# Router of a mixture of experts: fewer, wider operations, another order before the branch, lower biases added at expert 24, flags read one at a time

## The reference, cut to what matters

```python
def moe(x, w_router, b_router, w_up, b_up, w_down, b_down):
    logits = (xt @ w_router + b_router).astype(jnp.float32)
    top_val, top_idx = lax.top_k(logits, TOP_K)
    gates = jax.nn.softmax(top_val, axis=-1).astype(x.dtype)
...
    def expert_block(args):
        tok, g, e = args
        hdn = x_pad[tok] @ w_up[e] + b_up[e]
        gate_h = jnp.minimum(hdn[:, :D_FF_2], SWIGLU_LIMIT)
        up_h = jnp.clip(hdn[:, D_FF_2:], -SWIGLU_LIMIT, SWIGLU_LIMIT)
        act = (up_h + 1.0) * gate_h * jax.nn.sigmoid(SWIGLU_ALPHA * gate_h)
        y = act @ w_down[e] + b_down[e]
        return y * g[:, None]
```

## Time and profile before

| | |
|---|---|
| median of 3 runs | 2517.97 us (2517.13 to 2519.25) |
| the profiled execution's own time | 2516.45 us |
| its span, first to last instruction | 2514.7 us |
| mean granted clock of TensorE | 0.981 |
| TensorE busy | 2357.4 us, 94% |
| VectorE busy | 594.2 us, 24% |
| ScalarE busy | 520.9 us, 21% |
| mean DMA rate | 239 GB/s |

### The profile page before, as it was taken

The page is one execution under the profiler, slowest core; times in us unless marked ns, Lnnn a source line. Parts: engine busy times, 40 slices in busy tenths (PEclk is TensorE's granted clock), DMA queues, the critical chain, the costliest instruction groups (busy, mean ns, idle before and its releaser), DMA issues.

```text
span 2514.7 us, 33890 instructions
## 1 busy us (share of the span) xinstructions
PE 2357.4 (94%) x14632; PEld 1725.4 (69%) x14632; DVE 594.2 (24%) x1698; ACT 520.9 (21%) x1223; POOL 45.9 (2%) x64
## 2 busy tenths in 40 slices
PE   6888999999999879999999978999999999999997
PEld 3676788888887667887868854565666555555556
DVE  2044410000005322001575321122222222222223
ACT  2254432210003333200444120111111111111112
POOL 0000200000000000000000000000000000000000
PEclk9999999999999989999999978999999999999999
DMA  8811321123323504444433446799999999999992
GB/s 341 334 68 39 118 77 69 67 72 133 152 79 134 201 34 188 146 165 151 152 133 131 188 183 273 296 426 427 426 427 427 427 426 427 426 427 426 427 427 99
DMA packets 42115, 601.61 MB, mean 239 GB/s; under 512 B 4672, under 2 KB 5184, under 8 KB 5600
## 3 DMA queue, kind: packets, MB, share of 16 engines
q1 hardware_dynamic: 41472, 593.30, 58.2%
q10 hardware_dynamic: 480, 5.97, 0.6%
HBM read 598.20 MB, written 1.05 MB: 238 GB/s over the span
## 4 chain that ended last, share of the span: by engine, by line
PE 79%; DMA 14%; DVE 3%; ACT 2%; issue 1%; POOL 0%; DVEq 0%; SPq 0%; POOLq 0%; PEldq 0%; ACTq 0%
PE PS L560 13%; PE PS L551 13%; PE PS L935 12%; PE PS L693 7%; PE PS L959 7%; DMA BIG<-in_w_up 6%; DMA RG<-in_w_up 6%; PE PS L442 4%; PE PS L541 3%; PE PS L877 2%; PE PS L971 2%; DMA SM<-in_w_up 1%; PE PS L498 1%; DMA RG<-in_w_ada 1%; PE PS L383 1%
## 5 line engine op out<-in xcount | busy, mean ns | idle before, releaser
L551 PE MATMUL PS<-HN,RG 128*128 128x256 f32 x1536 | 333.9, 380 | 4.0 <-ACT HN L1145 4.0
L560 PE MATMUL PS<-BIG,RG 128*128 128x256 f32 x1536 | 333.1, 379 | 0.0
L551 PEld LDWEIGHTS PS<-HN,RG 128*128 128x128 f32 x1536 | 292.8, 191 | 44.6 <-issue 4.6
L560 PEld LDWEIGHTS PS<-BIG,RG 128*128 128x128 f32 x1536 | 291.4, 190 | 42.8 <-issue 3.4
L935 PE MATMUL PS<-BIG,XS 128*64 128x256 f32 (+1 forms) x2016 | 236.7, 384 | 10.1 <-DMA BIG<-in_w_up 10.0
L935 PEld LDWEIGHTS PS<-BIG,XS 128*64 128x64 f32 (+1 forms) x2016 | 145.0, 138 | 100.1 <-issue 17.2
L1100 ACT ACTIVATE BIG<-PS 128x256 f32<-128x256 f32 (+1 forms) x247 | 102.4, 422 | 520.1 <-PE PS L551 243.8
L2008 DVE TENSOR_SCALAR STAT<-PS 128x128 f32<-128x128 f32 (+1 forms) x128 | 37.9, 296 | 679.1 <-PE PS L935 679.1
L935 PE MATMUL PS<-RG,XS 128*64 128x256 f32 (+1 forms) x1520 | 182.9, 391 | 8.5 <-DMA RG<-in_w_up 8.5
L693 PE MATMUL PS<-XS,RG 128*128 128x256 f32 x768 | 172.1, 382 | 5.0 <-DVE XS L1617 4.1
L935 PEld LDWEIGHTS PS<-RG,XS 128*64 128x64 f32 (+1 forms) x1520 | 110.1, 140 | 80.7 <-issue 18.0
(11 more groups left out here) (291 smaller groups left out, 2340.1 us busy)
## 6 DMA issues: line engine op xcount, KB each, us to landing
BIG<-in_w_up SPq DMA_DIRECT2D x64, 2048.0 KB, 31.7
RG<-in_w_up SPq DMA_DIRECT2D x48, 2048.0 KB, 32.3
RG<-in_w_ff SPq DMA_DIRECT2D x32, 2048.0 KB, 8.3
BIG<-in_w_down SPq DMA_DIRECT2D x32, 2048.0 KB, 33.2
RG<-in_w_ada SPq DMA_DIRECT2D x24, 2048.0 KB, 9.1
RG<-in_w_down SPq DMA_DIRECT2D x24, 2048.0 KB, 33.8
RG<-in_w_in SPq DMA_DIRECT2D x23, 2048.0 KB, 8.0
SM<-in_w_up SPq DMA_DIRECT2D x16, 2048.0 KB, 31.7
```

The lines of the kernel that those rows point to most:

```text
L551: m = pe.matmul(banks[b][:, 0:256], w[:, k, 128 * n:128 * n + 128], own(HN, s)[:, k, :], start=k == 0, stop=k == 7)
L560: m = pe.matmul(banks[b][:, 0:256], w[:, k, :], own(FFH, s)[:, k, :], start=k == 0, stop=k == 31)
```

## The change

- **Halves together.** VectorE takes both token halves in one operation of 64 elements where the operation allows; `max`, the scan and the tie-breaking operation are still issued per half, but with one wait for the two. ScalarE's two exponentials wait once.
- **Order on TensorE.** Behind the logits come the `ht` transposes, then `pos` (which waits for the masks alone), then the transposes of the gates. `lg`, `pos` and `gt` lie in banks 0 to 2, `ht` in 4 to 7. `pos` is four matmul calls instead of five: two of those against `MSK[:, 0]` are one with 64 columns.
- **First gather ahead of the branch.** `select(0)`, `gather(0)`, `gather_turn(0)` and ScalarE's evacuations of them stand ahead of the fork. VectorE makes the flags behind `select(0)`.
- **Lower biases.** The eight matmuls of L841 leave the router; the scatter of expert 0 now starts the accumulators, and the biases are added at the start of expert 24. (In `dense` they stay ahead of the experts.)
- **Flags.** Ahead of the fork each engine reads `over` and the flag of expert 0. At the start of each expert it reads the flag of the next, into one of two registers.

SyncE's and GpSimd's programs do not change. The core of the diff:

```diff
+            F.pool, F.turn = [0, 1, 2, 3], 0
             b = take(("lg",))
...
-            b = take(("gt",))
-            for tt in range(2):
-                pe.wait_ge(s_gts, tt + 1)
-                m = pe.transpose(banks[b][0:32, tt * 128:tt * 128 + 128], GTE[:, tt, :], ID2)
-            read_out(("gt",))
-            for d in range(8):
-                pe.matmul(accap(d), BD[0:32, d * 128:d * 128 + 128], GTT, start=d % 2 == 0, stop=False, skip_group_check=True)
+            pos_bank, gt_bank = take(("pos",)), take(("gt",))
             F.pool, F.turn = [4, 5, 6, 7], 0
...
+            pe.wait_ge(s_sm3, 48)
+            pe.wait_ge(s_msk, 1)
+            b = pos_bank
+            pe.matmul(banks[b][:, 0:32], TRI, MSK[:, 0, :], start=True, stop=True)
+            pe.matmul(banks[b][:, 32:96], ONE1, MSK[:, 0:1, :].broadcast_to([128, 2, 32]), start=True, stop=False)
+            pe.matmul(banks[b][:, 32:64], TRI, MSK[:, 1, :], start=False, stop=False)
+            pe.matmul(banks[b][:, 64:96], ONE1, MSK[:, 1, :], start=False, stop=True).then_inc(s_full[b], 1)
+            b = gt_bank
+            pe.wait_ge(s_gts, 1)
...
+            def biases():
+                for d in range(8):
+                    pe.matmul(accap(d), BD[0:32, d * 128:d * 128 + 128], GTT, start=False, stop=False, skip_group_check=True)
             def expert(ex, broad):
+                if ex + 1 < NEXP:
+                    pe.load(wide[(ex + 1) % 2], FLAG[0:1, ex + 1:ex + 2])
+                if ex == BIASES:
+                    biases()
+            for tt in range(2):
+                for half in range(2):
+                    read_out(("ht", tt, half))
+            gather(0)
+            pe.wait_ge(s_flag, 1)
+            read_out(("pos",))
+            read_out(("gt",))
+            pe.load(over, FLAG[0:1, 32:33])
+            pe.load(wide[0], FLAG[0:1, 0:1])
+            gather_turn(0)
             pe.br_cmp(over, 0, on_true="pe_sparse", on_false="pe_dense", comp_op="IS_EQ")
```

and on VectorE:

```diff
-            for tt in range(2):
-                step(dve.max(M8[:, tt, :], LGT[:, tt, :]))
...
+            for tt in range(2):
+                D.up(dve.max(M8[:, tt, :], LGT[:, tt, :]))
+            dve.wait_ge(s_dve, D.n)
+            dve.tensor_scalar(c4b[:, :, 2:3], v1, -1.0, None, ALU.mult).then_inc(s_rmx, 1)
+            step(dve.tensor_tensor(MSK, LGT, v4, ALU.is_gt))
+            D.up(dve.tensor_reduce(c4b[:, :, 0], MSK, AX.X, ALU.add))
+            step(dve.tensor_tensor(EQ, LGT, v4, ALU.is_equal))
+            D.up(dve.tensor_scalar(c4b[:, :, 1:2], c4b[:, :, 0:1], -1.0, 4.0, ALU.mult, ALU.add))
...
+            dve.tensor_tensor(MSK, MSK, EQ, ALU.add).then_inc(s_msk, 1)
+            dve.wait_ge(s_rex, 2)
...
+            b = full(("pos",))
+            step(dve.tensor_copy(SV[:, 0:64], banks[b][:, 0:64]))
+            select(0)
...
```

More of the change, by code:

```diff
@@ L856, in _ @@
                     m.then_inc(s_full[b], 1)
[L857 to L860, removed]
+            pe.wait_ge(s_sm3, 48)
[8 more added lines that the diff above has]
+            for tt in range(2):
+                m = pe.transpose(banks[b][0:32, tt * 128:tt * 128 + 128], GTE[:, tt, :], ID2)
+            m.then_inc(s_full[b], 1)
+            wide = [pe.alloc_register(f"pe_wide{i}") for i in range(2)]
             over = pe.alloc_register("pe_over")
-            pe.load(wide, FLAG[0:1, 0:32])
-            pe.load(over, FLAG[0:1, 32:33])
             ended = list(F.at)
@@ L970, in expert @@
                             lh = YV[rows, c * 256 + (j // 2) * 128:c * 256 + (j // 2) * 128 + 128]
-                        m = pe.matmul(accap(d), lh, SCT[rows, :], start=False, stop=ex == NEXP - 1, skip_group_check=True)
+                        m = pe.matmul(accap(d), lh, SCT[rows, :], start=ex == 0 and d % 2 == 0, stop=ex == NEXP - 1,
+                                      skip_group_check=True)
                 m.then_inc(s_scat, 1)
@@ L1010, in _ @@
             with nc.body("pe_sparse", valid_engines=[mybir.EngineType.PE]):
-                for tt in range(2):
-                    for half in range(2):
-                        read_out(("ht", tt, half))
-                gather(0)
-                gather_turn(0)
                 ahead = []
@@ L1072, in _ @@
             with nc.body("pe_dense", parent=fork, valid_engines=[mybir.EngineType.PE]):
+                for b in range(4, 8):
+                    pe.wait_ge(s_free[b], taken[b])
+                for d in range(8):
+                    pe.matmul(accap(d), BD[0:32, d * 128:d * 128 + 128], GTT, start=d % 2 == 0, stop=False, skip_group_check=True)
                 for ex in range(NEXP):
@@ L1457, in _ @@
                     evac(HTM[:, tt, 512 * half:512 * half + 512], ("ht", tt, half), part=slice(0, 512))
-            act.wait_ge(s_flag, 1)
-            freed(("pos",))
-            wide = [act.alloc_register(f"act_wide{i}") for i in range(NEXP)]
+            evac(GTT, ("gt",), rows=slice(0, 32))
+            wide = [act.alloc_register(f"act_wide{i}") for i in range(2)]
             over = act.alloc_register("act_over")
-            act.load(wide, FLAG[0:1, 0:32])
-            act.load(over, FLAG[0:1, 32:33])
             def gathered(ex):
@@ L1494, in dense @@
                     act.activation(SG[:, f % 2, :], GH[:, f % 2, :], ACT.Sigmoid, scale=1.702).then_inc(s_dsg, 1)
+            gathered(0)
+            act.wait_ge(s_flag, 1)
+            freed(("pos",))
+            act.load(over, FLAG[0:1, 32:33])
+            act.load(wide[0], FLAG[0:1, 0:1])
             fork = nc.cur_bb
@@ L1956, in _ @@
-            dve.tensor_scalar(FLAG[0:1, 32:33], SV[0:1, 410:411], 128.0, None, ALU.is_gt).then_inc(s_flag, 1)
-            dve.tensor_scalar(FLAG[0:1, 0:32], banks[b][0:1, 64:96], 64.0, None, ALU.is_gt).then_inc(s_free[b], 1)
-            wide = [dve.alloc_register(f"dve_wide{i}") for i in range(NEXP)]
-            over = dve.alloc_register("dve_over")
-            dve.wait_ge(s_flag, 1)
-            freed(("pos",))
-            dve.load(wide, FLAG[0:1, 0:32])
-            dve.load(over, FLAG[0:1, 32:33])
@@ L2045, in dense @@
                     dve.tensor_tensor(ACTT[:, f, :], uh, sg, ALU.mult).then_inc(s_dact, 1)
+            b = full(("pos",))
+            dve.wait_ge(s_gts, 1)
+            step(dve.tensor_copy(SV[:, 0:64], banks[b][:, 0:64]))
+            dve.wait_ge(s_sm3, 48)
+            select(0)
+            step(dve.tensor_reduce(SV[0:1, 410:411], banks[b][0:1, 64:96], AX.X, ALU.max))
+            dve.tensor_scalar(FLAG[0:1, 32:33], SV[0:1, 410:411], 128.0, None, ALU.is_gt).then_inc(s_flag, 1)
+            dve.tensor_scalar(FLAG[0:1, 0:32], banks[b][0:1, 64:96], 64.0, None, ALU.is_gt).then_inc(s_free[b], 1)
+            dve.wait_ge(s_flag, 1)
+            freed(("pos",))
+            dve.load(over, FLAG[0:1, 32:33])
+            dve.load(wide[0], FLAG[0:1, 0:1])
+            D = Steps(s_dvef)
             fork = nc.cur_bb
```

62 lines of the change are left out of this document (23 added, 39 removed).

## The result

The changed kernel takes 2502.53 us (median of 6 runs, 2499.08 to 2509.12), the kernel before 2518.95 us (6 runs, 2517.13 to 2523.89). The ratio is 0.9937, 95% interval 0.9919 to 0.9956: some 16 us faster. 2502.6 was forecast.

The account below looks back on a forecast made before the run. Weight DMA was taken as the bound, its last unbroken stream starting after the router. Path saving 16.5 less clock 2.4 and reads 0.3 gave 13.8 us; 2516.45 - 13.8 = 2502.65 us, range 2497 to 2507.

Parts of the forecast that it names:

- The bound: Weight DMA sets the pace from about 1604 us; moving TensorE's first use of weights moves the end by the same amount.
- The order of the new path: Steps from logits' end to expert 0's first matmul: some 12.7 us instead of 29.2, 16.5 us saved.
- VectorE's masks and gates: Joined halves: masks about 2.3 us, then four steps to the gates, all under the transposes; VectorE saves about 1.8.
- the fork: Branch directly before expert 0, hidden under turning and evacuation; a stalled-fork rival had 4.0 us showing, 2506.6 us, chance 0.12.
- durations in that stretch are those at half clock: Between logits and expert 0 the clock is 1.2 GHz, so the old trace's durations were used for the new path.
- The early-clock rival: Clock back in the transposes or never falling, expert 0 starting at full: 20.4 us gained, 2496.1 us; chance 0.12.
- The clock term: Expert 0 starts at 1.2 GHz: 1.9 us lost on its first 64 records, 0.5 on the upper bias, 2.4 in all.
- The reads: Flag reads at most 0.09 us each; one each in experts 0, 1 and 2 before the stream, 0.3 us lost.
- The dear-read rival: A single read costs almost 2.97 us, TensorE becomes the bound at each expert's start: 2570 us; chance 0.04.
- The biases: Lower biases at expert 24: about 3.6 us at full clock, 7.16 at half, costing nothing at the end.
- The cover: Slack of the expert loop, since weights hold TensorE back: 28.8 us in all, of which biases and reads use 6.2.
- The sum: 16.5 less 2.4 for clock and 0.3 for reads: 13.8 us gained, set against the profiled execution's 2516.45.

Follow-up runs that it names:

- busy_in_gaps: Changed kernel plus 16 transposes into an unused PSUM bank, in TensorE's gaps around the first gather and turning; 2500.19 us, 0.9934 of the kernel before.
- the control: The changed kernel run again with no edit, for comparison with the other follow-ups; 2500.98 us, 0.9938 of the kernel before.

## Why the prediction came out as it did

- **The bound: right.** The router lies in a hole of the weight stream, and the stream's start sets the end. Thirteen traces agree to 3 us over 910, with bias matmuls behind the stream's start and without.
- **The order of the new path: right, its sizes too large.** I had expert 0 at 12.7 us behind the logits; it is 9.5. VectorE's masks and gates were within 0.3 us of the estimate, the fork free as said. The step that failed is "durations in that stretch are those at half clock": the clock came back at the end of the transposes in all but one of the twelve traces with this order. The early-clock rival had that half right: `pos` took 1.16 instead of 1.9, the gather 1.94 instead of 3.68, the turning 0.66 instead of 1.2.
- **The clock term: right in kind.** Expert 0 began at full clock and lost it at once: 1.7 us on the first chunk, for 2.4 in all. So neither my case nor the early-clock rival took place whole, but the front half of one and the back half of the other. busy_in_gaps shows that with the gaps filled there is no fall.
- **The reads: mis-sized.** "No trace shows a read by itself" was wrong: the trace of before has one, 0.32 us long, behind the instruction that reads the 32 others in 2.32 with its wait. So a single read costs 0.30 to 0.32, not 0.09, and the average of 0.09 holds only for many read in one instruction. Three would be 0.9 us instead of 0.3. Of these the one ahead of expert 0 lies under the turning and the evacuation; those of experts 1 and 2 run from 1516.67 to 1516.98 and from 1579.70 to 1580.00, right in front of their first matmuls (1517.14 and 1580.17), in stretches of issue that take 5.78 and 4.43 (5.89 and 4.97 in the second trace) against 5.87 and 4.80 before; whether 0.3 of each is the read's cannot be told from them. The dear-read rival, at 0.9 us and more for each, is out.
- **The biases: right.** 4.5 us instead of 3.6, and 2.5 more by the fallen clock, all covered; in the control's trace 3.7 and 1.7. The cover was counted as 28.8 us; 5 to 7 were used.
- **The sum.** From logits to stream the gain was 20.4 us in the first pair of traces, for 13.8 forecast: half as much again. By the second upper bias of expert 0, 18.1 of it was won (18.81 behind the logits instead of 36.88); the other 2.3 arose in expert 1, which the sum had at nothing: its turning, upper bias and first chunk took 0.66, 1.28 and 8.63 instead of 1.12, 2.08 and 9.05, its gather 0.2 less, and its two stretches of issue 0.5 less. That the early-clock rival's total was also 20.4 is chance, since its clock did not hold. The median came out within 0.1 us because two things made up for it. I subtracted from one execution's 2516.45, while the kernel's median was 2518.0 then and 2519.0 over six runs; and the moment at which the logits end, which I took as fixed, spreads over 8 us from run to run. By medians the gain was 16.4 and 15.7; why the traces show 18 to 20 behind the logits and the medians 16 stays open with a single trace of before. The hit on 2502.6 is luckier than the working deserves; the range was about right.
- **What I had not priced:** that the entry into expert 1 can take one fetch or two, 3.8 us apart. It changed when one instruction per block was taken out. The changed kernel was on the cheap side of that, as the kernel before was.

## What to carry to other kernels

Where a stream of loads sets the end, look for the last moment at which it stands still, and measure everything from the phase before it: work ahead of that moment counts in full, work behind it is free up to the slack, so move it there. Move it by the shortest chain of what must come first, and count the clock anew, since a stretch that gets shorter and more broken does not keep its old durations. Where blocks of code are chosen at run time, the path taken most should lie in one line, and a change that alters the length of code should be timed against another that alters it alike. And before a null result of an experiment that adds work is believed, the added instructions should be found in its trace: here they were not there.

## What the runs showed of the hardware

- Entering expert 1's broad block on TensorE costs 5.3 to 6.2 us of issue in ten traces with the broad blocks at the end of the program, 5.70 where it alone stands directly behind its narrow block, 7.07 where all do, and 9.6 and 9.7 in the two kernels in which a second block of instructions is fetched between the branch and the first matmul (123 in all instead of 122). The Trainium skill ("Runtime: NRT & Kernel Launch", Instruction fetch mechanics) says that instructions come in blocks of 16 KiB and that a taken branch to a block not held waits for its fetch. The traces agree: 2.00 MB in 122 packets are 16.4 KB each.
- One flag read into a register takes 0.30 us on TensorE's queue (31 reads, 0.297 to 0.318), 32 in one instruction 2.15. Under queued matmuls the single read does not show (27.87 us per expert with and without).
- Matmuls of 32 columns, TensorE busy without a gap: the granted clock fell to 1.2 GHz in them in 14 traces of 14 (0.53 in the window at 1469). It was back at the end of the transposes directly behind them in 11 traces of 12; in the kernel before the same transposes, behind the biases, ran at 1.2 GHz and the clock came back 8 us later.
- The eight matmuls with 32 rows of weights at expert 24: in six of ten traces the clock fell in them or in the chunk behind (8.80 to 9.54 us), in four it held (7.13).
